# A decoder trunk's first loads and its attention loop: input transposed tile by tile, first weights in two column parts, and ScalarE and VectorE put in another order

## The reference

```python
h = x @ w_in + b_in                       # layer 0, even mixer: 1024 -> 1536
y_a = s5_branch(h[..., :512], ...)        # state-space groups
y_b = conv_branch(h[..., 512:], ...)      # gated depthwise convolution
...
q, kc, vc, ks, vs, kw, vw, gl = split(x @ w_in)      # layer 1: sparse attention
p_c = masked_softmax(q @ k_cmp)           # 31 compressed keys
p_s = masked_softmax(q @ k_sel)           # selected blocks (all 8 fit into the 16 that may be chosen)
p_w = masked_softmax(q @ k_win)           # sliding window of 512
o = g0 * p_c @ v_cmp + g1 * p_s @ v_sel + g2 * p_w @ v_win
```

## Time and profile before

| | us |
|---|---|
| median of 3 runs (2122.98 to 2125.33) | 2124.73 |
| the profiled execution, its own time | 2123.23 |
| its span in the trace | 2121.2 |
| first projection, first x tile to the barrier | 1.2 to 113.3 |
| attention, first score to last copy | 1152.2 to 1339.9 |

### The profile page before, as it was taken

One profiled execution on the slowest core, in us unless ns is written; L12 is line 12 of the kernel. 1 busy time (PEld: TensorE's weight loads), 2 busy tenths in 40 slices (PEclk: granted clock), 3 DMA queues, 4 the chain that ended last, 5 costly groups with the idle time before them and its releaser, 6 DMA issues. The chain is left out here.

```text
span 2121.2 us, 26424 instructions
## 1 busy us (share of the span) xinstructions
PE 1990.8 (94%) x8534; PEld 989.3 (47%) x8534; DVE 746.5 (35%) x1929; ACT 400.1 (19%) x890; POOL 394.7 (19%) x381
## 2 busy tenths in 40 slices
PE   8998998999999999978998898998999999999977
PEld 4553454444444444433446565554444444444433
DVE  3683352222222222216432566343222222222216
ACT  2103021111111111101002566111111111111110
POOL 0000200111111111100110778500111111111110
PEclk9999999999999999999998899999999999999998
DMA  6132245999999999958402000226899999999957
GB/s 227 11 53 113 111 190 212 400 407 412 406 409 388 412 396 386 401 229 352 78 0 80 1 2 2 105 77 266 334 407 402 417 406 411 399 412 400 406 220 332
DMA packets 107426, 566.01 MB, mean 267 GB/s; under 512 B 38625, under 2 KB 39393, under 8 KB 69089
## 3 DMA queue, kind: packets, MB, share of 16 engines
q1 hardware_dynamic: 79136, 497.99, 59.1%
q0 software_dynamic: 28224, 67.16, 8.1%
HBM read 539.78 MB, written 59.77 MB: 283 GB/s over the span
## 5 line engine op out<-in xcount | busy, mean ns | idle before, releaser
L439 PE MATMUL moe_bank<-moe_weights,moe_xgT 128*128 128x512 f32 x1024 | 457.0, 599 | 15.5 <-DMA moe_weights<-in_ex_weights 15.1
L439 PEld LDWEIGHTS moe_bank<-moe_weights,moe_xgT 128*128 128x128 f32 x1024 | 190.0, 190 | 232.2 <-issue 215.9
L315 POOL DMA_INDIRECT y<-moe_xy,moe_rows x98 | 98.6, 1006 | 945.2 <-DVE moe_idx L757 569.1
L777 DVE TENSOR_TENSOR moe_hid<-moe_sil,moe_bank 128x256 f32<-128x256 f32 x98 | 41.3, 421 | 661.1 <-ACT moe_sil L640 661.1
L472 PE MATMUL moe_bank<-moe_weights,moe_hidT 128*128 128x512 f32 x512 | 230.5, 593 | 0.0
L442 PE MATMUL moe_bank<-moe_weights,moe_xgT 128*64 128x512 f32 x512 | 226.6, 595 | 0.0
L442 PE MATMUL moe_bank<-wide,moe_xgT 128*64 128x512 f32 x512 | 226.6, 595 | 0.0
L640 ACT ACTIVATE moe_sil<-moe_bank 128x256 f32<-128x256 f32 x98 | 37.6, 383 | 657.4 <-PE moe_bank L439 456.0
L785 DVE TENSOR_SCALAR moe_xy<-moe_bank,moe_sgate 128x512 f32<-128x512 f32 x98 | 73.6, 751 | 219.5 <-PE moe_bank L472 142.1
L300 POOL DMA_INDIRECT moe_xy<-h,moe_idx x98 | 99.9, 1019 | 267.1 <-DVE moe_idx L757 239.5
L1847 POOL TENSOR_SCALAR att_prob<-att_prob,att_coef 128x128 f32<-128x128 f32 (+3 forms) x128 | 136.7, 1089 | 60.6 <-DVE att_coef L2015 37.8
(11 more groups left out here) (353 smaller groups left out, 2432.8 us busy)
## 6 DMA issues: line engine op xcount, KB each, us to landing
moe_weights<-in_ex_weights SPq DMA_DIRECT2D x96, 2048.0 KB, 19.6
moe_weights<-in_ex_weights SPq DMA_DIRECT2D x96, 1024.0 KB, 19.2
wide<-in_ex_weights SPq DMA_DIRECT2D x34, 2048.0 KB, 22.0
wide<-in_ex_weights SPq DMA_DIRECT2D x34, 1024.0 KB
moe_weights<-y SPq DMA_DIRECT2D x18, 1024.0 KB, 20.7
wide<-y SPq DMA_DIRECT2D x8, 1024.0 KB, 7.9
moe_xy<-y SPq DMA_DIRECT2D x6, 1024.0 KB, 27.0
oddin_win<-in_od_w_in_heads SPq DMA_DIRECT2D x1, 4288.0 KB, 18.7
```

The lines of the kernel that those rows point to most:

```text
L315: pool.indirect_dma_start(out=y_dram[:, :], out_offset=IndirectOffsetOnAxis(ap=rows[k][:, 0:1], axis=0), in_=y[k], in_offset=None, bounds_ ...
L439: mm = pe.matmul(bG[:, :], xgT[:, n, :], wgu[j][:, :, n, :], start=(n == 0), stop=(n == KC - 1))
```

## The change

It has three edits.

1. Loads and transposes of the first projection. Each x tile gets its own semaphore; PE transposes tile by tile (8 transposes into two banks, four banks in turns), and ACT copies chunks 0 to 3 and DVE chunks 4 to 7 of each tile. The first weight block of 512 columns is loaded as two transfers of 256 columns (1 MB each), the first of them ahead of the table of columns. PE waits for the first before product 0 and for the second before product 2.
2. ACT's and DVE's order in the attention. The copies are of unit k-3 in iteration k (they were of k-2), and lie between the other work: DVE does masks 0 and 1, copy 1, masks 2 and 3, coefficients, copy 3; ACT does copy 0, exponentials 0 and 1, the compressed copy, copy 2, exponentials 2 and 3. PE's order isn't changed.
3. The output copy of a group is on ACT one iteration later, and both loops run one iteration more. DVE's `coefficients` waits for its own last one.

```diff
@@ even_in_project @@
-                sp.dma_start(g.x[:, i, :], w["x"][0, i * P:(i + 1) * P, :]).then_inc(g.x_loaded, 16)
+                sp.dma_start(g.x[:, i, :], w["x"][0, i * P:(i + 1) * P, :]).then_inc(x_loaded[i], 16)
+            src = w["ev_w_in"][0].rearrange("(p c) f -> p c f", c=KC)
+            sp.dma_start(win[0][:, :, 0:2 * P], src[:, :, 0:2 * P]).then_inc(first_landed, 16)
             sp.dma_start(e.cols[:], w["columns"]).then_inc(cols_loaded, 16)
...
             for k in (0, 2, 1):
-                sp.dma_start(win[k], src[:, :, k * 512:(k + 1) * 512]).then_inc(win_landed[k], 16)
+                lo = 0 if k else 2 * P
+                sp.dma_start(win[k][:, :, lo:], src[:, :, k * 512 + lo:(k + 1) * 512]).then_inc(win_landed[k], 16)
...
-            pe.wait_ge(g.x_loaded, 64)
-            emit_transposes(pe, g.x, g.c["ident"], bank[0:2], xt_done, (xt_a, xt_v))
+            for i in range(NT):
+                pe.wait_ge(x_loaded[i], 16)
+                if i >= 2:
+                    pe.wait_ge(xt_a, i - 1)
+                    pe.wait_ge(xt_v, i - 1)
+                for n in range(KC):
+                    mm = pe.transpose(bank[2 * (i % 2) + n // 4][:, (n % 4) * P:(n % 4 + 1) * P],
+                                      g.x[:, i, :].rearrange("t (k c) -> t c k", c=KC)[:, n, :], g.c["ident"])
+                mm.then_inc(xt_done, 1)
...
-                if n in (0, 4, 5):
+                if n == 0:
+                    pe.wait_ge(first_landed, 16)
+                if n in (2, 4, 5):
                     pe.wait_ge(win_landed[f // 4], 16)
...
-            for k in range(0, KC, 2):
-                act.wait_ge(xt_done, k + 1)
-                act.activation(g.xT[:, k, :], bank[0][:, :], ACT.Copy).then_inc(xt_a, 1)
+            for i in range(NT):
+                act.wait_ge(xt_done, i + 1)
+                act.activation(g.xT[:, 0:4, i * P:(i + 1) * P], bank[2 * (i % 2)][:, :].rearrange("p (k t) -> p k t", k=4), ACT.Copy).then_inc(xt_a, 1)
@@ attention, ACT @@
+            for k in range(units + 5):
+                turned = 3 <= k <= units + 2
+                if turned:
+                    take_turn(act, copy, k - 3, 0).then_inc(evac_a, 1)
                 if k < units:
+                    exponentials(k, (0, 1))
+                if turned:
+                    for d in c_turns(k - 1):
...
+                    take_turn(act, copy, k - 3, 2).then_inc(evac_a, 1)
+                if k < units:
+                    exponentials(k, (2, 3))
...
-                if k >= 7 and k % NT == 3:
-                    d = k // NT - 1
+                if k >= 8 and k % NT == 0:
+                    d = k // NT - 2
@@ attention, DVE @@
                 dve.wait_ge(exp_ready, 4 * n + 4)
+                if n:
+                    dve.wait_ge(coef_ready, n)
...
                         compressed_low(d, c)
+                if 3 <= k <= units + 2:
+                    take_turn(dve, dve.tensor_copy, k - 3, 1).then_inc(evac_v, 1)
+                if k < units:
                     dve.wait_ge(win_done, k + 1)
                     mask(k, 2)
                     mask(k, 3)
...
-                if k >= 2:
-                    take_turn(dve, dve.tensor_copy, k - 2, 1).then_inc(evac_v, 1)
-                    take_turn(dve, dve.tensor_copy, k - 2, 3).then_inc(evac_v, 1)
+                if k >= 3:
+                    take_turn(dve, dve.tensor_copy, k - 3, 3).then_inc(evac_v, 1)
```

More of the change, by code:

```diff
@@ L1235, in _ @@
         def _(dve):
-            for k in range(1, KC, 2):
-                dve.wait_ge(xt_done, k + 1)
-                dve.tensor_copy(g.xT[:, k, :], bank[1][:, :]).then_inc(xt_v, 1)
+            for i in range(NT):
+                dve.wait_ge(xt_done, i + 1)
+                dve.tensor_copy(g.xT[:, 4:8, i * P:(i + 1) * P], bank[2 * (i % 2) + 1][:, :].rearrange("p (k t) -> p k t", k=4)).then_inc(xt_v, 1)
             link = lambda ins: dve_steps.link(dve, ins)
@@ L1945, in _, with exponentials @@
             copy = lambda out, in_: act.activation(out, in_, ACT.Copy)
-            for k in range(units + 4):
-                if k < units:
[L1948 to L1954, removed]
-                    for d in hosted(k):
-                        act.wait_ge(c_shifted, d + 1)
-                        flat = cp[d % 2][:].rearrange("p i h n -> p (i h n)")
-                        act.activation(flat, flat, ACT.Exp, scale=-1.0).then_inc(c_exp, 1)
-                if 2 <= k <= units + 1:
-                    take_turn(act, copy, k - 2, 0).then_inc(evac_a, 1)
-                    for d in c_turns(k):
+            def exponentials(k, hbs):
+                for hb in hbs:
+                    width = (where(k)[2] + 1) * P
+                    act.wait_ge(masked, 4 * k + hb + 1)
+                    if k >= 2 and hb == 0:
+                        act.wait_ge(coef_ready, k - 1)
+                    act.activation(prob[k % 4][:, hb, 0:width], prob[k % 4][:, hb, 0:width], ACT.Exp, scale=-1.0,
+                                   bias=low[k % 2][:, hb:hb + 1], accum_out=total[k % 2][:, hb:hb + 1]).then_inc(exp_ready, 1)
+            for k in range(units + 5):
+                turned = 3 <= k <= units + 2
+                if turned:
+                    take_turn(act, copy, k - 3, 0).then_inc(evac_a, 1)
+                if k < units:
+                    exponentials(k, (0, 1))
+                if turned:
+                    for d in c_turns(k - 1):
                         turn = turn_of["c", d]
@@ L1966, in _ @@
                         copy(cpT[d % 2][:, :], bT[turn % 2][0:64, :]).then_inc(evac_a, 1)
-                    take_turn(act, copy, k - 2, 2).then_inc(evac_a, 1)
-                if k >= 7 and k % NT == 3:
-                    d = k // NT - 1
+                    take_turn(act, copy, k - 3, 2).then_inc(evac_a, 1)
+                if k < units:
+                    exponentials(k, (2, 3))
+                    for d in hosted(k):
+                        act.wait_ge(c_shifted, d + 1)
+                        flat = cp[d % 2][:].rearrange("p i h n -> p (i h n)")
+                        act.activation(flat, flat, ACT.Exp, scale=-1.0).then_inc(c_exp, 1)
+                if k >= 8 and k % NT == 0:
+                    d = k // NT - 2
                     pair, j, _ = where(NT * d)
@@ L2020, in _ @@
             dve.wait_ge(gate_ready, 1)
-            for k in range(units + 2):
+            for k in range(units + 3):
                 if k < units:
```

4 lines of the change are left out of this document (2 added, 2 removed).

## The result

The changed kernel took 2111.66 us (median of 20 runs, 2105.44 to 2125.26), the kernel before 2122.64 (20 runs, 2117.11 to 2126.66). The ratio is 0.9949, with a 95% interval of 0.9939 to 0.9960: 11.0 us less, where 10.1 were forecast. The forecast of the time itself was 2114.6; of the 2.9 us between it and the median, 2.1 are the median of before, which was taken as 2124.73 from three runs, and 0.9 are the gain. The profiled execution of the changed kernel is one of the longer ones: its own time is 2117.03, its span 2115.0.

A forecast was written before the change was run, and what follows sets the result against it. PE was taken to bound the kernel, in the first projection and the attention's steady part. 4.9 + 1.5 + 1.6 + 2.1 = 10.1 us less, from 2124.73 to 2114.6; own range 2112 to 2117.5, whole range 2108.5 to 2119.5.

The forecast's parts named there:

- First projection: Start of the kernel: the first product starts at 12.7 us where it started at 17.57, 4.9 us less.
- The rival that it starts cold: First projection: clock rises only after products begin, 2.8 us of the 4.9 are lost, 2117.4; chance 0.1.
- Steady part: Attention's repeating period of 21.19 us: 0.3 less a period, 1.5 us less over five full periods.
- the compressed turn: Attention period: PE's compressed turn still waits for ACT's copy 0, now first in its iteration, about 0.3 us.
- turn 3 behind the compressed copy: Attention period: turn 3 needs the bank emptied by ACT's compressed copy, behind two wide exponentials; wait 0.45 us.
- copy 1 behind the compressed steps: Attention, unit of width 256: turn 3 needs DVE's copy 1, behind two masks and three compressed steps; wait 1.1 us.
- copy 3 behind the scaling steps: Attention, widest unit: turn 1 needs copy 3 of the unit before, behind four scaling steps; wait 0.25 us.
- The removed waits: Attention period: five PE waits of 1.93 us go, about 2.5 counted from when PE could have issued.
- Fill: Attention's start: PE's 1.60 wait for masks goes, 1.6 us less, if the 10.1 us at clock 0.50 stay.
- The clock rival: Attention's fill: the clock doesn't fall, 4 us more are gained, 2110.5; chance 0.25.
- Drain: Attention's end: POOL's last stretch begins 10.8 us after unit 27's scores instead of 12.9, 2.1 us less.
- The slower rival: Attention: sel scores still wait for masks, 2127.5; sign: copy 1 ends later than the window scores; chance 0.05.

The follow-up runs named there:

- experiment 8: The kernel of experiment 4 with 28 unused transposes added between the real ones and the first product: 2116.01 us, ratio 0.9977 to the kernel before.
- experiment 4: The changed kernel with the first weight block of 512 columns loaded whole, ahead of the table of columns: 2116.99 us, ratio 0.9982 to the kernel before.
- experiment 5: The changed kernel with ACT's attention order of before, DVE keeping the new order: 2113.85 us, ratio 0.9957 to the kernel before.
- experiment 9: The changed kernel with DVE's copy 1 ahead of the compressed steps and ACT's order of before: 2102.1 us, ratio 0.9901 to the kernel before.
- experiment 3: The changed kernel with DVE's copy 1 ahead of the three compressed steps: 2104.64 us, ratio 0.9919 to the kernel before.
- experiment 10: The kernel of experiment 9 with DVE's copy 3 also ahead of the four scaling steps: 2102.93 us, ratio 0.9912 to the kernel before.
- experiment 7: The kernel of experiment 3 with copy 3 ahead of the scaling steps and ACT's compressed copy between exponentials 0 and 1: 2101.76 us, ratio 0.9894.
- experiment 2: The changed kernel with the first projection of before, keeping only the attention and output copy changes: 2115.51 us, ratio 0.9978 to the kernel before.
- experiment 1: The changed kernel with the whole attention of before, keeping only the first projection's change: 2115.82 us, ratio 0.9974 to the kernel before.
- experiment 6: The changed kernel with DVE's copy 1 behind all four masks: 2151.81 us, ratio 1.0128 to the kernel before.

## Why the prediction was right, and where it wasn't

**First projection, right.** Forecast 4.9, measured 4.96. The first tile lands at 5.13 and no later one holds PE up; the transposes were ready sooner (10.7, not 11.9), so that the weights end the wait: 12.59 against 12.7. That the two agree hides two errors: against 12.1 the megabyte is 0.5 late, for the queue did not keep its 390 GB/s with pieces of 1 KB but moved 365 and 349, and the transposes, which were to set the start, are 1.2 early. In the eight profiles with the column halves the first product begins between 12.10 and 12.85.

The rival that it starts cold fell: the 64 products take 27.70, in all eight. The change's trace also bears out that transposes bring the clock up. PE does nothing but transposes until 10.7, and their mean falls from 424 ns in the stretch from 5 to 7 us to 283 in the one from 8.7 to 11 (275 in the 28 of experiment 8, at a granted clock of 1.00; columns as in the earlier trace rows):

```profile
L1157 PE MATMUL evin_bank<-const_sb,x_sb 128*128 128x128 f32 x9 | 2.2, 424 | 5.1 <-DMA x_sb<-in_x 5.1
...
L1157 PE MATMUL evin_bank<-const_sb,x_sb 128*128 128x128 f32 x17 | 2.3, 283 | 0.0
```

The first clock record in this trace is a rise to the full level at 8.5 us; before it the view gives 1.00 even while PE hasn't begun, so there the durations tell more than the clock column. But the rival's danger was real and near. PE now stops for 1.88 before the first product, which the prediction said wouldn't happen ("PE would now stop for nothing"); with 3.42 the clock is lost (experiment 4), with 0.83 to 1.96 (the eight profiles) and with 1.25 (experiment 8) it wasn't. This is also what the column halves are for: without them, in the profile of experiment 4, edit 1 gains nothing. Experiments 4 and 8 differ by 28 transposes alone, and in their rows the granted clock behind the wait is 0.50 without them and 1.00 with them. The Trainium skill (TensorE: Matmul & The Clock Gate, section on PE-mode transpose) says that transposes don't engage the full clock; these rows speak against it, for raising the clock as for holding it.

**Steady part, right in sum: about 20.9 forecast (21.18 less 0.3), 20.86 measured.** The four new waits, forecast and as the trace shows them: the compressed turn 0.3 and 0.35; turn 3 behind the compressed copy 0.45 and 0.29 (0.37 in time by experiment 5, 0.50 by experiment 9); copy 1 behind the compressed steps 1.1 and 0.91 (1.1 in time, experiment 3); copy 3 behind the scaling steps 0.25, and there is none (all five waits on DVE's copies in the change are on copy 1, and experiment 10 moves copy 3 and the period stays). The removed waits: a period with no wait but the 0.35 is 19.28, 1.9 less than before; the prediction had 2.5 - 0.3 = 2.2. The new waits that went with experiments 7 and 9 come to 20.86 - 19.28 = 1.58, where the prediction had 1.8. So it was in part luck: errors of 0.3 and 0.2 cancelled, and where the prediction's own terms gave 2.5 - 2.1 = 0.4 less a period, it took 0.3 without a reason; measured is 0.32.

**What the prediction left out: the clock in the steady part.** It had the clock as a rival in the fill and in the first projection alone, and at nothing in the steady part. The new wait of 0.91 is longer than any of before (0.81 at most) and lies among narrow units; in the profiles with this attention code the clock fell right behind it in 1 period of 5 here, 1 of 5 in experiment 2, 2 of 5 in experiment 8 and none in experiment 4, for 1.6 to 3.1 us each. Experiment 5 has the same wait in five periods, and no fall: in all, 4 falls behind 25 such waits. No period of the kernel before or of experiments 1, 3, 7, 9 and 10, 30 in all, is longer than the others, and in experiment 6, with waits up to 1.71, four of five have a fall. It fits the spread of the runs: 12 runs with this attention code spread over 16 to 18 us (experiments 2, 4 and 8), 12 with that of before over 10 (experiment 1), and the change's slowest run of 20, 2125.26, has a mean granted clock of 0.971, its fastest, 2105.44, of 0.980. But the clock of a run is known over its whole span only, and no run's time was traced to these waits.

**Fill, right in sign, mis-sized.** Forecast 1.6, measured 2.9 in the changed kernel's profile and 7.6 to 8.0 in the two with the short fill. Its condition, that the 10.1 us at a granted clock of 0.50 stay as they are, was the step that failed: in the changed kernel's profile the clock is at 0.50 from 14 to 31 us after the first scores without the rise that it had before at 20 to 24, and in the two short fills it is full from 18 us on. The wait of 1.60 went as forecast (sel scores of unit 4 come straight behind turns at 1167.59). The clock rival, 4 us more and a chance of 0.25, is what happens in some executions: the short fills are 4.7 to 5.1 shorter. It was not a question of which case holds but of how often. Why an execution takes the one or the other isn't settled. Other orders have both too: 33.81 and 34.76 in experiments 3 and 7, 40.36, 40.35 and 35.62 in experiments 5, 9 and 10, the three with ACT's old order.

**Drain, right.** Forecast 2.1, measured 1.97 (2.1 in experiments 2, 4 and 8); POOL's stretch begins 10.8 after unit 27's scores, as worked out.

**The slower rival** fell: it needed PE's sel scores to wait for masks still, and the change has no such wait in its steady part. Its sign, copy 1 ending later than the window scores, holds clearly in one unit of four. Experiment 6 brings the sign about in all four, and is 1.3% slower than before, but by waits on the copy and by the clock; the rival's own mechanism, waits for masks, isn't seen there either.

**The sum.** 10.1 forecast, 11.0 measured by medians. The first projection and the drain are right term by term. The rest agrees in part by luck: in every profile with this attention code the fill gave more than its term (2.9 to 8.0 against 1.6), and clock falls in the steady part, which had no term, took 0 to 6.2 back. In these four profiles the whole attention is 4.8, 9.8, 6.7 and 5.5 shorter than before (the change, experiments 2, 4 and 8); the forecast was 5.2.

## What to carry to other kernels

A copy that frees a bank for the bottleneck engine belongs ahead of work that nobody waits for yet: the same edit with one copy three instructions earlier gave 17 us less instead of 11 less, and 20 with ACT's order left as it was. When a change reorders two engines, try each alone; here one of the two reorderings cost 0.37 a period and was hidden by what the other gained. Before moving a load or an engine's start, look at how long that engine would sit idle behind it: here 3.42 us of waiting cost 2.7 more in clock, and in one execution unused transposes in the gap brought that part back, though the medians can't tell.

## What the runs showed of the hardware

A wait of 3.42 us between transposes and products brought the granted clock of TensorE from 1.00 to 0.50 and cost 2.7 us more in the products behind; waits of 0.83 to 1.96 at the same place, in nine executions, did not. Transposes alone brought the clock up (424 to 283 ns each), and 28 of them held it at 1.00 in the gap. Within the attention, a wait of 0.91 was followed by a fall in some periods and not in others, in the same execution and with the same instructions: the rows 1208.09 and 1249.80 above are two such periods. So for this wait the clock costs between nothing and 3.1 us a time, the rows don't show what decides it, and a single profile doesn't tell its mean.

With the transfers of 256 columns, in pieces of 1 KB, on it, the queue moved 365 GB/s from 9 to 12 us and 349 from 12 to 15 (352 and 351 in experiment 1); with those of 512 columns, in pieces of 2 KB, it moved 400 and 386 before and 377 to 399 in experiments 4 and 8. That is far from the 107 GB/s of the worst row. And the unchanged layers between the first stage and the attention took from 1034.3 to 1040.8 us in profiles of kernels that have the same code there, a difference of 6.5 us, where the change brings 11.
